# Expert weights in two halves: 96 transfers of 2 MB become 192 of 1 MB, each half with its own semaphore

## The reference, cut to what matters

```python
def expert_block(args):
    e, tok, g = args
    xb = ht[tok]
    hid = jax.nn.silu(xb @ w1[e]) * (xb @ w3[e])
    return (hid @ w2[e]) * g[:, None].astype(ht.dtype)
```

## Time and profile before

| | us |
|---|---|
| median of 3 runs | 1719.24 |
| lowest, highest | 1718.75, 1721.62 |
| the profiled execution's own time | 1722.07 |
| its span in the profile | 1720.3 |
| PE busy (matmuls, ends modelled) | 1412.8 |
| DVE busy | 1079.6 |
| ACT busy | 681.6 |
| expert stage of layer 0, from the first split to the last output copy | 509.1 to 938.7 |
| expert stage of layer 1, the same | 1332.9 to 1682.9 |

### The profile page before, as it was taken

One profiled execution on the slowest core, in us unless ns is written; L12 is line 12 of the kernel. 1 busy time (PEld: TensorE's weight loads), 2 busy tenths in 40 slices (PEclk: granted clock), 3 DMA queues, 4 the chain that ended last, 5 costly groups with the idle time before them and its releaser, 6 DMA issues. The chain is left out here.

```text
span 1720.3 us, 20595 instructions
## 1 busy us (share of the span) xinstructions
PE 1412.8 (82%) x6658; PEld 988.3 (57%) x6659; DVE 1079.6 (63%) x1228; ACT 681.6 (40%) x759; POOL 131.5 (8%) x112
## 2 busy tenths in 40 slices
PE   3888999379828999999996299799993699999981
PEld 2454555134426888877885244488542487778770
DVE  2189999954476884776541812376436678887834
ACT  3201101041116764676441500166311577777732
POOL 0000000000001111111110200000000011112101
PEclk9999999689958999999998599799996799999995
DMA  9356564220039997697671700220102899999954
GB/s 329 115 204 244 176 216 169 110 76 37 25 122 325 385 397 269 255 382 270 235 298 73 294 20 0 57 43 2 38 37 73 309 360 393 381 379 376 389 207 183
DMA packets 154157, 354.91 MB, mean 206 GB/s; under 512 B 6161, under 2 KB 23297, under 8 KB 154113
## 3 DMA queue, kind: packets, MB, share of 16 engines
q1 hardware_dynamic: 137584, 298.68, 47.9%
q0 software_dynamic: 8784, 31.99, 5.2%
q10 hardware_dynamic: 7744, 23.68, 3.4%
HBM read 318.57 MB, written 35.75 MB: 206 GB/s over the span
## 5 line engine op out<-in xcount | busy, mean ns | idle before, releaser
L1346 DVE TENSOR_TENSOR W_LO<-WRAW,W_HI 128x2048 fp32r<-128x2048 f32 x192 | 430.9, 2287 | 165.9 <-ACT W_HI L1270 165.9
L1270 ACT ACTIVATE W_HI<-WRAW 128x2048 fp32r<-128x2048 f32 x192 | 356.8, 1908 | 190.9 <-DMA WRAW<-in_moe_w 151.7
L1207 PE MATMUL PS<-W_HI,XLO 128*128 128x512 f32 x624 | 255.1, 409 | 36.1 <-DVE XLO L1355 36.1
L1209 PE MATMUL PS<-W_HI,XHI 128*128 128x512 f32 x624 | 249.0, 399 | 0.0
L1208 PE MATMUL PS<-W_LO,XHI 128*128 128x512 f32 x624 | 247.7, 397 | 0.0
L972 PE MATMUL PS<-HT,RING 128*128 128x512 f32 (+1 forms) x512 | 173.1, 494 | 6.8 <-DVEq L1043 6.8
L1207 PEld LDWEIGHTS PS<-W_HI,XLO 128*128 128x128 f32 x624 | 120.4, 193 | 69.2 <-issue 40.0
L972 PEld LDWEIGHTS PS<-HT,RING 128*128 128x128 f32 x512 | 96.5, 192 | 85.7 <-issue 72.3
L1209 PEld LDWEIGHTS PS<-W_HI,XHI 128*128 128x128 f32 x624 | 119.8, 192 | 26.7
L1207 PE MATMUL PS<-W_HI,HLO 128*128 128x512 f32 x312 | 126.5, 405 | 10.0 <-DVE HLO L1367 9.5
L1208 PEld LDWEIGHTS PS<-W_LO,XHI 128*128 128x128 f32 x624 | 120.7, 193 | 24.0
(11 more groups left out here) (225 smaller groups left out, 1652.3 us busy)
## 6 DMA issues: line engine op xcount, KB each, us to landing
WRAW<-in_moe_w SPq DMA_DIRECT2D x96, 2048.0 KB, 11.9
RING<-in_w_mod SPq DMA_DIRECT2D x24, 2048.0 KB, 14.3
moe_out<-YO ACTq DMA_DIRECT2D x39, 512.0 KB, 6.8
RING<-in_conv_pw SPq DMA_DIRECT2D x16, 512.0 KB, 5.3
moe_out<-NIL SPq DMA_DIRECT2D x15, 512.0 KB, 13.4
ROWS<-rows_of_layer SPq DMA_DIRECT2D x12, 512.0 KB, 6.1
RING<-in_attn_w_qkv SPq DMA_DIRECT2D x3, 2048.0 KB, 16.1
moe_in<-RING SPq DMA_DIRECT2D x10, 512.0 KB, 2.6
```

The lines of the kernel that those rows point to most:

```text
L1207: pe.matmul(to, lo, W_HI[:, q, at:at + 512], start=start, stop=False)
L1209: return pe.matmul(to, hi, W_HI[:, q, at:at + 512], start=False, stop=stop)
L1270: nc.scalar.activation(part(W_HI, q, p), part(WRAW, q, p), ACT.Copy).then_inc((w2_hi if q == 2 else w_hi)[L], 1)
L1346: nc.vector.tensor_tensor(part(W_LO, q, p), part(WRAW, q, p), part(W_HI, q, p).bitcast(F32), ALU.subtract).then_inc(lo[L], 1)
```

## The change

Each fetch of a weight is issued as two transfers, one for each half of its k tiles. Each half has its own semaphore, in place of one for each weight. ACT waits for its engine's condition on `W_HI` first, then before each half of the split for that half alone. The count that it waits for is the same, 16 for each load. Nothing else changes: the buffers, SP's waits, the sizes of the splits and the order on each engine are as they were.

```diff
-        w1_in = both("w1_in")
-        w3_in = both("w3_in")
-        w2_in = both("w2_in")
+        w1_in = [both(f"w1_half{p}_in")[0] for p in range(2)]
+        w3_in = [both(f"w3_half{p}_in")[0] for p in range(2)]
+        w2_in = [both(f"w2_half{p}_in")[0] for p in range(2)]
...
-                sp.dma_start(WRAW[:, q, :].rearrange("p (k f) -> p k f", k=FE // P if q == 2 else KT),
-                             src[bass.ds(e, 1)].rearrange("e p k f -> p (e k) f")).then_inc(
-                                 (w1_in, w3_in, w2_in)[q][L], 16)
+                kn = FE // P if q == 2 else KT
+                for p in range(2):
+                    half = slice(p * kn // 2, (p + 1) * kn // 2)
+                    sp.dma_start(WRAW[:, q, :].rearrange("p (k f) -> p k f", k=kn)[:, half, :],
+                                 src[bass.ds(e, 1)].rearrange("e p k f -> p (e k) f")[:, half, :]).then_inc(
+                                     (w1_in, w3_in, w2_in)[q][p], 16)
...
-                        act.wait_ge(landed[L], load * 16 + 16)
                         if not first(b):
                             act.wait_ge(used[L], b)
                         for p in range(2):
+                            act.wait_ge(landed[p], load * 16 + 16)
                             nc.scalar.activation(part(W_HI, q, p), part(WRAW, q, p), ACT.Copy).then_inc(
```

## The result

| | before | changed |
|---|---|---|
| median, us | 1718.99 (4 runs, 1717.42 to 1721.62) | 1695.63 (4 runs, 1694.35 to 1696.53) |
| profiled execution, us | 1722.07 | 1694.35 |
| its span, us | 1720.3 | 1692.5 |
| ratio to before, 95% interval | | 0.9861, 0.9846 to 0.9875 |

The forecast was 1705.7 with a range from 1697 to 1716. The time is 23.4 us less by the medians, where 13.5 were forecast; it lies 1.4 us under the range, next to the rival "more than forecast" (1696.5). Run once more in a later series the changed kernel took 1696.82 us (1694.15 to 1699.03, 6 runs), 0.9860 of the kernel before.

What follows compares the result with a forecast made beforehand. PE (17.7 us a block) and DMA (18.4) were taken as nearly equal bounds, with PE waiting for `XLO`. 12.7 + 1.5 - 0.2 - 0.5 = 13.5 us less than 1719.24 gave 1705.7, range 1697 to 1716.

Steps and rivals of the forecast that it cites:

- more than forecast: Rival: layer 1 reaches layer 0's pace (8 us) and the clock stays up in one start (2.7); 22.7 us less, chance 0.10.
- The chain: From w1's landing through ACT's and DVE's split to `HID` and `XLO`: 4.2 us after full landing in place of 6.44.
- slots freed earlier: SP issues each next weight up to 2.2 us sooner; in layer 1 worth 1.5 us, bounds 0 and 8.
- GB/s in full stretches unchanged: Sign of being right: the DMA rate where DMA engines are full stays as before; below 376 was a sign of wrong.
- a pace other than 19.1: Sign of being wrong: layer 1's blocks take a time other than 19.1 us each.
- Block 9 to 15 of layer 0: Window 713 to 785 in the prediction: PE loses 3.3 us there, 2.2 of it comes back.
- The starts: Block 1 of each layer: `XLO`, PE and the next w1's issue 2.2 us earlier; two layers, 4.4 us.
- the clock: PE at half pace after idle time in block 1: taken as nothing, bounds +4.4 lost to -5.4 for two layers.
- 568 to 641: DMA-bound window of layer 0, two blocks at 18.4 in place of 17.7: 1.1 us to come back.
- 785 to 910: Layer 0's three pairs of blocks: loop shorter by 2.2 us a pair falls below PE's pace, 2.8 us back.
- More transfers: 96 added transfers: issue cost on SP hidden, DMA boundaries cost 0.2 us in all.
- ACT's waits: Added wait between ACT's halves: some 0.1 us at five places, 0.5 us; 9.6 if ACT had no slack.

Runs made afterwards that it cites:

- either aid alone: Changed kernel with four register loads on SP before each issue: 1701.95 us; or with ACT awaiting both halves, SP issuing w1/w3 halves once DVE read them: 1701.64 us.
- the smaller transfers alone: Changed kernel, but ACT waits for both halves before its first half of the split: 1714.83 us, 0.9969 of before.
- Free halves: Changed kernel, and SP issues the first half of w1 and w3 as soon as DVE has read that half: 1694.43 us, 0.9848 of before.
- the kernel with the later gather: Kernel before the change, with six register loads on POOL ahead of each gather: 1723.69 us, 1.0006 of before.
- the one with layer 0 alone: The change in layer 0 only, layer 1 fetching its weights whole as before: 1710.15 us, 0.9926 of before.

## Why the prediction was wrong, point by point

**The chain: right.** The two halves land 2.7 us apart, and in layer 1 ACT's halves start 2.7 apart (1467.35, 1470.06). From the second half's start to DVE's `HID` it is 4.2 us (1470.06 to 1474.22), as worked out. The changed kernel in order of time, ACT and DVE:

```profile
1467.35 1.92 ACT L1273 ACTIVATE W_HI<-WRAW 128x2048 fp32r<-128x2048 f32 x1 [0.97 <-DMA WRAW<-in_moe_w]
1470.06 1.92 ACT L1273 ACTIVATE W_HI<-WRAW 128x2048 fp32r<-128x2048 f32 x1 [0.79 <-DMA WRAW<-in_moe_w]
...
1472.01 2.29 DVE L1349 TENSOR_TENSOR W_LO<-WRAW,W_HI 128x2048 fp32r<-128x2048 f32 x1 [0.42 <-ACT W_HI L1273]
1474.22 0.68 DVE L1366 TENSOR_TENSOR HID<-PS,SIL 128x512 f32<-128x512 f32 x1
```

**The step that failed: "slots freed earlier".** The term was mis-sized, and its reason was wrong. I took 1.5 us of bounds from 0 to 8, "since most of the gap comes as lower GB/s in busy engines, which an earlier issue doesn't mend". It does mend it: with either aid alone the window 1440 to 1497 moves 398 GB/s, and with neither 388. From block 3 to 15 of layer 1 the change brought 10.3 us (10.8 in the second profile), where 2.2 + 1.5 were forecast, and the pace went from 19.11 to 18.39: the upper bound of 8 us, in full. A busy share of 1.01 at 376 GB/s was read as full engines that happen to be slow; the traces show a hand-over from w2 to w1, in eight of the blocks 4 to 15, at which the flow falls for some microseconds. "GB/s in full stretches unchanged" was among its signs of being right and did not come; a pace other than 19.1 was among its signs of being wrong and did. The rival "more than forecast" had this term, 8 us and layer 0's pace, and a chance of 0.10. That its total of 22.7 lies next to the 23.4 of the medians is in part luck, since the starts and block 9 to 15 brought more than it had and block 3 to 9 less. The first and last `XLO` of the stretch with its 11 blocks:

```profile
1401.51 1.22 DVE L1358 TENSOR_TENSOR XLO<-PS,XHI 128x1024 fp32r<-128x1024 f32 x1
...
1603.76 1.22 DVE L1358 TENSOR_TENSOR XLO<-PS,XHI 128x1024 fp32r<-128x1024 f32 x1
```

Block 9 to 15 of layer 0 is the same in small: its window had 377 GB/s, and gave 5.8 us where I counted 2.2. There the smaller transfers alone brought 3.5, and 398 GB/s.

**The starts: too small, and the clock with them.** 4.4 us were forecast, 9.4 came (8.3 in the second profile). `XLO` of block 1 is 2.5 us sooner in layer 0, as forecast, and block 2 and 3 add 1.3 and 1.1. The clock was taken as nothing between bounds of 4.4 lost and 5.4 gained; the stretch at the lower level is 3.4 us shorter in each layer, and time at half pace loses at most half of itself, 1.7 us each. Free halves gives a hint of its worth in layer 0: it has the same 2.5 and 1.1 us in block 1 and 3 as the changed kernel, but its low stretch is 6.8 us, as before, and block 2 brings nothing in place of 1.3. So the clock is worth some 1.4 us there. What the rest of the starts owes to the earlier issue was not measured by itself. The prediction's bound of 2.7 us a layer is half of the 5.4 us that PE was busy in its window, and that window holds 13 products, not the 24 it names.

**568 to 641: nothing in place of 1.1.** It was at 398 GB/s already; `XLO` keeps its 18.4 us a block, and PE's small loss vanished from the window without moving the end.

**785 to 910: 2.8 forecast, 2.8 measured.** But the reason was half right: the kernel that waits for both halves has it too, so there the smaller transfers suffice.

**More transfers: right.** No pause at boundaries: 1 MB pieces move at 398 GB/s, and w1 alone in halves has the pace of all in halves. The Trainium skill's page "DMA: Bandwidth & Descriptors" has under "Anatomy of one DMA" the fit that the prediction used, made for GpSimd's path; worked out for 1 MB it gives, as an estimate, 4.4 us. Read as time in series this is not what the queued transfers of this trace show: their halves land 2.7 us apart.

**ACT's waits: right in size.** Its split costs 362.6 us in place of 356.8, 5.8 more of the 9.6 at most, and none of it shows in the chain.

**Open** is what exactly slows the flow to 335 GB/s in a slow block. The lead sorts most blocks: in the kernel before, the kernel with the later gather and the one with layer 0 alone, all 24 blocks at 3.7 to 3.8 us took 19.05 to 20.67. But three of the twelve at 5.0 to 5.1 us there took 19.2 to 19.5, and with halves one at 3.75 took 18.4. And the lead is counted to the landing on the last of the 16 DMA engines: in the kernel before the first of them was done with w2 only 1.3 to 2.6 us after w1's issue, in slow and clean blocks alike, and the last up to 3.8 us behind it. That slack at the hand-over is what decides is shown by adding and taking it away; how a short lead lowers the rate was only argued.

## What to carry to other kernels

- Where the same work moves at 377 GB/s in one stretch and at 398 in another, the difference is a price to be explained, not a property of the stretch. Look for when the next transfer is issued against the landing of the one ahead, block by block; means hide an alternation.
- A chain between a landing and the next issue that is a little too long is paid for at every load (here 1.9 us of each further 2.2, some 60 us over 32 loads), while within the slack the same 2.2 us cost the pace nothing. Take the upper bound seriously where the row's rate lies below the best rate in the same trace.
- Splitting a transfer pays through what may start earlier, here 19 of 24 us; the smaller transfers alone gave 4.7. Of those 19 an earlier free buffer can bring 13 without the early half.

## What the runs showed of the hardware that was not expected

- A core's DMA engines show a busy share of 1.01 to 1.03 and yet move 5% less than at 1.04 (376 to 393 against 398 GB/s). The share does not tell the two apart; the rate does.
- Another four register loads before each issue, some 2.2 us, from 5.1 us of lead on, cost some 60 us (1701.95 to 1761.00).
- POOL's index copy ahead of the gather follows PE with 13.80 or 16.00 us of idle time in turn, in the kernel before, and so the gather goes out 1.9 or 4.1 to 5.2 us before `XLO`. The kernel before, in order of time:

```profile
1492.21 0.18 POOL L1188 COPY icur<-IDX 128x1 uint32 x1 [13.80 <-PE PS L1201]
1493.14 2.87 POOL L1176 DMA_INDIRECT XG<-moe_in,icur  x1 [0.75 <-POOL icur L1188]
1512.02 1.60 POOL L1188 COPY icur<-IDX 128x1 uint32 x1 [16.00 <-PE PS L1201]
1514.37 2.25 POOL L1176 DMA_INDIRECT XG<-moe_in,icur  x1 [0.75 <-POOL icur L1188]
```
